# Down projection's biases in a mixture of experts: added once to each token's row of sums instead of once in each block

## The chip, the cores and the metric

One core of one Trainium2 chip runs the whole program in one launch. The metric is the device time of that launch in microseconds. The core has TensorE (PE, with its weight loads shown apart as PEld), VectorE (DVE), ScalarE (ACT), GpSimd (POOL), SyncE (SP), and 16 DMA engines that serve the queues of SP, ACT and POOL.

## What is computed

The reference is two transformer blocks on 512 tokens of width 1024. The change lies in the last part, the mixture of experts (32 experts, each token goes to 4 of them, hidden width 1024):

```python
def moe_ffn(h, w_router, b_router, w_gate_up, b_gate_up, w_down, b_down):
    logits = jnp.dot(h, w_router, ...) + b_router
    top_logit, top_idx = lax.top_k(logits, TOP_K)              # TOP_K = 4
    gate = jax.nn.softmax(top_logit, axis=-1)
    ...                                                        # slots: 128 rows of one expert make a block
    def expert_block(args):
        tok, g, e = args
        xb = h_pad[tok]
        gu = xb @ w_gate_up[e] + b_gate_up[e]
        y = clamped_swiglu(gu) @ w_down[e] + b_down[e]
        return y * g[:, None].astype(y.dtype)
    y = lax.map(expert_block, ...)
    out = jnp.zeros((n_tok + 1, d), y.dtype).at[slot_tok].add(y.reshape(n_slots, d))
    return out[:n_tok]
```

A token's output is therefore the sum over its four experts of gate times (down projection plus b_down of that expert), and the bias part of it is the gates' sum of b_down, which depends on the routing alone.

## The kernel before

Everything is float32. A product is made of three: each operand is split into a high part (ACT, a copy rounded to fp32r) and a low part (DVE, the rest), and high·high, low·high and high·low are added up in PSUM. That is the `k` and `part` loops of `half` in `experts_pe`.

**Up to the loop.** The two blocks' layers take the time up to about 1240 us. Then the router's results are turned into lists: DVE works out each slot's place (`tail_dve`), PE's 16 products of group "lists" put tokens and gates of all slots into one tile, DVE copies them out as `list_tok` and `list_gate`, and POOL (`experts_pool`) gathers the first two blocks' rows with an indirect DMA (`rows_of`) and fetches lists (`take_list`, two tiny copies and a `drain`). A DRAM tensor `acc_dram` (in the trace: acc_rows) holds a row of sums for every token; five DMAs of 512 KB of zeros, issued by POOL near the start of the program, clear it. `b_split` is the biases of all experts (gate, up and down, 3072 columns, experts as partitions, high parts in 32 rows and low parts in the next 32), which `bias_sp`, `bias_act` and `bias_pool` make long before the loop. `bias_pool` also clears the four row buffers `xgy`, of which the first two (`xg`) take gathered rows and the last two (`y_sb`) a block's results.

**The loop.** It runs 32 blocks of 128 slots, two per pass (`Fori(0, n)`), on all five engines at once. A block's weights are six 1024x512 quarters of two halves each: 12 halves of 1 MB. For each half, SP loads it into `raw` (a ring of 6), ACT copies the high part into `w_split` (a ring of 4, so it waits until PE is through with the half four before: semaphore half_used), DVE subtracts to get the low part, and PE does 12 products of 512 columns (`half`). The order of the halves is the table TURN: two halves each of gate and up for the first 512 hidden columns and then the second 512, and the down projection's halves between them: `run(6)`, `run(7)`, `run(10)` and `run(11)` are the down projection's, in PSUM banks 4 and 5, `run(8)` and `run(9)` already the next block's first.

Around the halves stand these steps, each waiting for another engine:

- `bias(j, s)` begins the sum in bank j with the expert's bias row: one product of 512 columns of `sel` (ones in the rows of the expert, made by `select` on DVE) with `b_split`. There are six a block: j = 0 to 3 for gate and up, 4 and 5 for down.
- After `run(5)` PE waits for the previous block's results to have been taken out of banks 4 and 5 (`ye_ready`), does `bias(4)` and `bias(5)`, and then waits until the first half of the hidden rows, turned, is split (`t_out`, DVE's `turned_low` with output hidden_T) before `run(6)`. Before `run(10)` it waits for the second half of them in the same way.
- ACT's queue has, besides the 12 high parts, two tanh (act_buf, L1360 and L1369), the high parts of turned rows (L1338), and `take_out` (L1341), which scales banks 4 and 5 by the gate into `y_sb`.
- DVE's queue has, besides the 12 low parts (L1381), the clamped gates (L1397), the hidden rows (L1401 to L1405), the low parts of turned rows (L1387) and `select` (L1392).
- POOL gathers rows for the block after the next and adds `y_sb` into `acc_dram` by an indirect DMA.

At the end SP reads `acc_dram` back and the last layer's norm follows.

Of the kernel before, what the change touches and what calls it, by code (L numbers as in the profile page):

```python
# [19 lines left out]
F32 = mybir.dt.float32  # L20
F32R = mybir.dt.float32r
# [12 lines left out]
P = 128  # L34
# [194 lines left out]
def build(nc, io):  # L229
    ctx = ExitStack()  # L230
    with ctx:
# [42 lines left out]
        empty = early.enter_context(nc.sbuf_tensor("empty", [P, LISTS], F32))  # L274
        early.close()
# [23 lines left out]
        xg, y_sb = xgy[:, 0:2, :], xgy[:, 2:4, :]  # L299
        b_raw = xgy[0:2 * E_N, 0:3, :].rearrange("p a b -> p (a b)")  # L300
# [128 lines left out]
        CV = Groups(nc, ctx, "cv", [0, 1, 2], [f"w{i}" for i in range(DK)] + ["pos", "be", "lists"])  # L429
        CA = Groups(nc, ctx, "ca", [3, 6, 7], [f"t{i}" for i in range(8)])  # L430
# [92 lines left out]
        SHIFT, SQ_SUM, LAST_GAINED, R_COL, CHOSEN, DIAG = range(1, 7)  # L523
# [3 lines left out]
        gate_exp, gate_d = sem("gate_exp"), sem("gate_d")  # L527
# [27 lines left out]
        def tail_pe(pe, mm):  # L555
# [237 lines left out]
            m.then_inc(CV.full, 1)  # L793
            experts_pe(pe, mm)
# [139 lines left out]
        def tail_dve(dve, inverse, rope):  # L934
# [222 lines left out]

            x = full(CV, "lists")[:, 0:2 * LISTS].rearrange("p (c b) -> p c b", c=2)
# [5 lines left out]
            dve.sem_inc(CV.free, 1)  # L1164
            experts_dve(dve)
# [39 lines left out]
        def bias_pool(pool):  # L1205
            pool.drain()
            nc.gpsimd.memset(b_split[2 * E_N:P, :].bitcast(F32), 0.0)
            pool.drain()
            pool.wait_ge(bias_high, 1)
            nc.gpsimd.tensor_tensor(b_split[E_N:2 * E_N, :], b_raw[E_N:2 * E_N, :],  # L1210
                                    b_split[E_N:2 * E_N, :].bitcast(F32), ALU.subtract).then_inc(bias_split, 1)
            pool.drain()
            nc.gpsimd.memset(xgy[:], 0.0)
            pool.drain()

        def experts_sp(sp):
# [3 lines left out]
            sp.wait_ge(CA.full, CA.n)  # L1220
# [22 lines left out]
        def experts_pe(pe, mm):  # L1243
# [18 lines left out]
            def half(n_, slot, j, q, s, inc=1):  # L1262
                rows = xgT[:, s] if j < 4 else hTe[:]
                w = wsp[:, slot % SPLIT]
                pe.wait_ge(high, n_ + 1)
                for k in range(4):
                    at_ = (4 * q + k) * P
                    for part in range(2):
                        mm(ps[:, j, :], rows[:, part, at_:at_ + P], w[:, 0, k * S:(k + 1) * S], False, False)
                pe.wait_ge(low, n_ + 3)  # L1270
                for k in range(4):
                    at_ = (4 * q + k) * P
                    m = mm(ps[:, j, :], rows[:, 0, at_:at_ + P], w[:, 1, k * S:(k + 1) * S], False,
                           q == 1 and k == 3)
                m.then_inc(used, inc)

            pe.wait_ge(bias_split, 1)
# [8 lines left out]
            with pe.Fori(0, n) as i:  # L1286
                for s in range(2):
# [23 lines left out]
                    bias(4, s)  # L1311
                    bias(5, s)
# [14 lines left out]
        def experts_act(act):  # L1327
# [16 lines left out]
            act.wait_ge(CA.full, CA.n)  # L1344
# [31 lines left out]
        def experts_dve(dve):  # L1376
# [62 lines left out]
        def experts_pool(pool):  # L1439
# [6 lines left out]
            pool.wait_ge(acc_init, 16 * (ACC_ROWS // P))  # L1446
# [30 lines left out]
            take_list(0, 0)  # L1477
            with pool.Fori(0, n) as i:
# [1148 lines left out]
        def _(pool):  # L2627
            def constants_in():
# [6 lines left out]
                for t in range(ACC_ROWS // P):  # L2635
                    pool.dma_start(acc_dram[1 + t * P:1 + (t + 1) * P, :], io["zeros"]).then_inc(acc_init, 16)
# [192 lines left out]
```

## Time and profile before

| | |
|---|---|
| median of 3 runs | 2475.66 us (2474.69 to 2476.12) |
| the profiled execution | 2474.83 us |
| its span in the trace | 2473.0 us |
| PE busy | 2400.4 us, 97% of the span |
| DVE busy | 2020.5 us, 82% |
| ACT busy | 1319.3 us, 53% |
| POOL busy | 689.3 us, 28% |
| weight load of PE (PEld) busy | 1938.1 us, 78% |
| the loop of 32 blocks | from about 1269 us to 2431 us |

The 1.8 us between span and time lie outside the traced span. An engine's busy time is the union of its instructions. Busy PE is not PE at its peak, since its products overlap: one of 512 columns is shown 0.39 us long and the next begins 0.23 us after it. The page's chain of the work that ended last puts 87% on PE; it follows an engine's own instructions wherever the wait ahead of one is small.

### The profile page before, as it was taken

How to read it: one execution, taken by the hardware profiler on the slowest of the kernel's cores; microseconds unless marked ns; L12 is line 12 of the kernel's file. 1: busy time of each engine (PE TensorE's matmuls, PEld its weight loads, DVE VectorE, ACT ScalarE, POOL GpSimd, SP SyncE). 2: the span in 40 equal slices, each digit the busy share in tenths (PEclk: the TensorE clock that was granted, in tenths of full speed). 3: DMA queues.
4: the chain of work that ended last, by engine and by line, in shares of the span. 5: the costliest groups of instructions: out<-in, count | busy, mean ns of one | idle time of the engine just before them, and what ended most of it. 6: DMA issues, size and time to landing. Idle time of an engine off the chain costs nothing.

```text
span 2473.0 us, 31635 instructions
## 1 busy us (share of the span) xinstructions
PE 2400.4 (97%) x10905; PEld 1938.1 (78%) x10905; DVE 2020.5 (82%) x1839; ACT 1319.3 (53%) x1207; POOL 689.3 (28%) x409
## 2 busy tenths in 40 slices
PE   8999999999999999999969999999999999999995
PEld 7777788777877877887858888888888888888883
DVE  7787577576885796887379999999999999999994
ACT  4442223334423234425357777777777777777772
POOL 5343251333433423342322112211211221122120
PEclk9999999999999998999989999999999999999998
DMA  6232246221422672320099999999999999999992
GB/s 240 86 120 77 68 146 203 69 77 68 145 61 76 223 262 64 108 94 27 13 323 370 370 372 370 372 367 377 366 366 373 368 371 373 373 364 366 375 361 90
DMA packets 105989, 574.55 MB, mean 232 GB/s; under 512 B 15241, under 2 KB 15401, under 8 KB 55850
## 3 DMA queue, kind: packets, MB, share of 16 engines
q1 hardware_dynamic: 87770, 515.16, 55.7%
q0 software_dynamic: 17856, 58.25, 8.4%
q8 instruction: 47, 0.77, 0.1%
q14 instruction: 28, 0.23, 0.0%
q10 hardware_dynamic: 288, 0.14, 0.0%
HBM read 561.43 MB, written 26.22 MB: 238 GB/s over the span
## 4 chain that ended last, share of the span: by engine, by line
PE 87%; DVE 7%; DVEq 1%; DMA 1%; issue 1%; ACT 1%; POOL 1%; ACTq 0%; SPq 0%; POOLq 0%
PE ps L1585 84%; PE ps L1250 2%; DVE scr L2446 1%; DVE scr L2286 1%; DVEq L2448 1%; POOL pieces_split L2641 0%; DMA scr<-in_ada 0%; PE ps L695 0%; DVE mix L2337 0%; DVE y_split L2223 0%; DVE scr L2335 0%; DMA mix<-acc_rows 0%; DMA acc_rows<-rows,lst 0%; DVE w_split L1381 0%; DMA rows<-h_rows,slot_tokens 0%
## 5 line engine op out<-in xcount | busy, mean ns | idle before, releaser
L1381 DVE TENSOR_TENSOR w_split<-raw,w_split 128x2048 fp32r<-128x2048 f32 x386 | 877.7, 2288 | 52.9 <-ACT w_split L1332 41.8
L1585 PE MATMUL ps<-y_split,pieces_split 128*128 128x512 f32 x3600 | 846.3, 396 | 16.2 <-POOLq L2653 7.4
L1332 ACT ACTIVATE w_split<-raw 128x2048 fp32r<-128x2048 f32 x386 | 736.3, 1917 | 192.7 <-PE ps L1585 176.4
L1585 PEld LDWEIGHTS ps<-y_split,pieces_split 128*128 128x128 f32 x3600 | 680.4, 190 | 168.1 <-issue 26.3
L1585 PE MATMUL ps<-w_split,rows_T 128*128 128x512 f32 x3096 | 751.8, 394 | 0.1
L1585 PEld LDWEIGHTS ps<-w_split,rows_T 128*128 128x128 f32 x3096 | 575.2, 188 | 117.5 <-DVE rows_T L1387 0.6
L2641 POOL TENSOR_TENSOR pieces_split<-pieces,pieces_split 128x1024 fp32r<-128x1024 f32 x151 | 371.9, 2474 | 649.9 <-ACT pieces_split L1919 519.8
L1919 ACT ACTIVATE pieces_split<-pieces 128x1024 fp32r<-128x1024 f32 x144 | 151.3, 1058 | 426.9 <-PE ps L1585 395.9
L1585 PE MATMUL ps<-w_split,hidden_T 128*128 128x512 f32 x1536 | 363.5, 392 | 1.8 <-DVE hidden_T L1387 1.7
L1585 PEld LDWEIGHTS ps<-w_split,hidden_T 128*128 128x128 f32 x1536 | 285.9, 188 | 71.9 <-DVE hidden_T L1387 13.2
L1456 POOL COPY rows_i<-slot_tokens 128x1 int32 x32 | 56.6, 1768 | 370.0 <-PE ps L1250 369.5
L1585 PE MATMUL ps<-scr 128*128 128x128 f32 (+3 forms) x576 | 137.6, 387 | 2.7 <-DVEq L991 1.7
L1470 POOL DMA_INDIRECT acc_rows<-rows,lst x33 | 65.4, 1981 | 229.9 <-ACT rows L1341 229.9
L1585 PE MATMUL ps<-pieces_split,y_split 128*128 128x512 f32 (+1 forms) x672 | 126.1, 348 | 0.0
L1585 PEld LDWEIGHTS ps<-scr 128*128 128x128 f32 x576 | 86.8, 191 | 46.4 <-issue 33.6
L1585 PEld LDWEIGHTS ps<-pieces_split,y_split 128*128 128x128 f32 x672 | 106.7, 190 | 16.2 <-issue 1.4
L1461 POOL COPY lst<-slot_tokens 128x1 int32 (+1 forms) x34 | 10.7, 314 | 309.1 <-DMA acc_rows<-rows,lst 303.4
L1450 POOL DMA_INDIRECT rows<-h_rows,rows_i x32 | 88.9, 2778 | 26.8 <-issue 26.8
L2208 DVE RECIPROCAL scr<-scr 128x512 f32<-128x512 f32 (+1 forms) x20 | 63.9, 3193 | 24.8 <-ACT scr L1868 21.1
L1938 ACT ACTIVATE mix<-ps 128x512 f32<-128x512 f32 x32 | 19.0, 594 | 106.3 <-DVE ps L2262 106.3
L2446 DVE SCALAR_TENSOR_TENSOR scr<-scr,cond 128x1024 f32<-128x1024 f32 x56 | 70.6, 1282 | 5.2 <-DMA scr<-in_ada 2.7
L1585 PE MATMUL ps<-bias_split,expert_rows 128*128 128x512 f32 x193 | 70.4, 392 | 0.0
(276 smaller groups left out, 2062.6 us busy)
## 6 DMA issues: line engine op xcount, KB each, us to landing
raw<-in_w_moe SPq DMA_DIRECT2D x386, 1024.0 KB, 7.4
pieces<-in_pieces SPq DMA_DIRECT2D x181, 512.0 KB, 3.5
scr<-in_ada POOLq DMA_DIRECT2D x48, 512.0 KB, 5.5
scr<-in_ple SPq DMA_DIRECT2D x2, 1536.0 KB, 7.1
acc_rows<-in_zeros POOLq DMA_DIRECT2D x5, 512.0 KB, 11.1
h_rows<-shift_row SPq DMA_DIRECT2D x1, 2052.0 KB
hT<-in_xT SPq DMA_DIRECT2D x8, 256.0 KB, 5.6
h_rows<-scr POOLq DMA_DIRECT2D x4, 512.0 KB, 7.7
```

The costliest lines, as they stand in the source:

```text
L1250: m = pe.transpose(ps[:, bank, j * P:(j + 1) * P], src[:, j * P:(j + 1) * P], ident[:])
L1332: nc.scalar.activation(wsp[:, p % SPLIT, 0], raw[:, p % RAW, :], ACT.Copy).then_inc(high, 3 if p == 1 else 1)
L1381: nc.vector.tensor_tensor(wsp[:, p % SPLIT, 1], raw[:, p % RAW, :], wsp[:, p % SPLIT, 0].bitcast(F32), ALU.subtract).then_inc(low, 3 if p ...
L1450: nc.gpsimd.indirect_dma_start(out=xg[:, s, :], out_offset=None, in_=h2_dram[:, :], in_offset=bass.IndirectOffsetOnAxis(ap=index.bitcast(U ...
L1456: nc.gpsimd.tensor_copy(rows_i[:, s:s + 1], list_tok[:, bass.ds(b, 1)])
L1470: nc.gpsimd.indirect_dma_start(out=acc_dram[:, :], out_offset=bass.IndirectOffsetOnAxis(ap=lst[:, s, 0:1].bitcast(U32), axis=0), in_=y_sb[ ...
L1585: return pe.matmul(out, lhsT, rhs, start=start, stop=stop)
L1919: nc.scalar.activation(wps[:, n % A_SPLIT, 0], pieces[:, place_of(after, at_), :], ACT.Copy).then_inc(p_high, 1)
L2208: nc.vector.reciprocal(r, r)
L2286: last = nc.vector.scalar_tensor_tensor(o, x[:, 1 + w:1 + w + S], p_("conv_w", w * LRU_T + i), o, ALU.mult, ALU.add)
L2446: last = nc.vector.scalar_tensor_tensor(out, aring[slot], c, out, ALU.mult, ALU.add)
L2641: nc.gpsimd.tensor_tensor(wps[:, n % A_SPLIT, 1], pieces[:, place_of(layer, at_), :], wps[:, n % A_SPLIT, 0].bitcast(F32), ALU.subtract).t ...
```

## The change

- Before the loop DVE multiplies the one-hot table of chosen experts by the gates and sums over the four choices, which gives a token's gate for every expert (`gate_of`, twice side by side). PE turns it (group "gates", four transposes), ACT and DVE split it into `gate_T`.
- PE then makes eight tiles of 128 tokens by 512 columns: gates times down's biases, two products each (group "z0" to "z7", three banks in turn). ACT copies each out into memory that is not in use yet: the two `y_sb` buffers, `h_sb` and `act_buf`.
- POOL writes these four 128x1024 tiles to `acc_dram`. Four of the five DMAs of zeros near the start are gone; one stays, for the rows past the tokens.
- ACT, DVE and POOL wait in front of the loop for all five writes to `acc_dram` (`acc_init`), ACT and DVE since the loop writes over the staging memory.
- In the loop `bias(4)` and `bias(5)` are gone; the first product of `run(6)` and of `run(7)` begins the sum. The wait for `ye_ready` stays.
- `bias_pool` clears only the two `xg` buffers.

```diff
@@ bias_pool
-            nc.gpsimd.memset(xgy[:], 0.0)
+            nc.gpsimd.memset(xg, 0.0)
@@ tail_pe, after group "lists"
+            g = "gates"
+            ...
+            for t in range(ST):
+                m = pe.transpose(ps[0:2 * E_N, CV.bank(g), t * P:(t + 1) * P], gate_of[:, t].rearrange("p c e -> p (c e)"),
+                                 ident[:])
+            m.then_inc(CV.full, 1)
+            pe.wait_ge(bias_split, 1)
+            pe.wait_ge(route_ready, GATES_LOW)
+            for i in range(8):
+                g, t = f"z{i}", i // 2
+                pe.wait_ge(CA.free, CA.reusable(0, g))
+                out, at_ = ps[:, CA.bank(g), :], 2 * D + (i % 2) * S
+                mm(out, gate_T[0:2 * E_N, 0, t * P:(t + 1) * P], b_split[0:2 * E_N, at_:at_ + S], True, False)
+                mm(out, gate_T[0:E_N, 1, t * P:(t + 1) * P], b_split[0:E_N, at_:at_ + S], False, True).then_inc(CA.full, 1)
@@ tail_dve, ahead of the lists' copies
+            nc.vector.tensor_tensor(hot2, hot, value[:, :, 1:2].to_broadcast([P, ST * TOP, E_N]), ALU.mult)
+            dve.drain()
+            nc.vector.reduce_sum(gate_of[:, :, 0, :], hot2.rearrange("p (t k) e -> p t e k", k=TOP), AX.X)
+            dve.drain()
+            nc.vector.tensor_copy(gate_of[:, :, 1, :], gate_of[:, :, 0, :])
+            dve.drain().then_inc(route_ready, 1)
@@ ... and behind them
+            dve.wait_ge(gate_high, 1)
+            nc.vector.tensor_tensor(gate_T[0:E_N, 1, :], ps[0:E_N, CV.bank("gates"), :],
+                                    gate_T[0:E_N, 0, :].bitcast(F32), ALU.subtract).then_inc(route_ready, 1)
@@ experts_pe
+                begins = j >= 4 and q == 0
                 ...
-                        mm(ps[:, j, :], rows[:, part, at_:at_ + P], w[:, 0, k * S:(k + 1) * S], False, False)
+                        mm(ps[:, j, :], rows[:, part, at_:at_ + P], w[:, 0, k * S:(k + 1) * S], begins and k + part == 0, False)
                 ...
                     pe.wait_ge(ye_ready, b + 1)
-                    bias(4, s)
-                    bias(5, s)
                     pe.wait_ge(t_out, 3 * b + 4)
@@ experts_act, ahead of the loop
-            for p in range(2):
-                high_part(p, p, (raw_in[p], 16))
+            high_part(0, 0, (raw_in[0], 16))
+            act.wait_ge(CV.full, CV.done(0, "gates"))
+            nc.scalar.activation(gate_T[0:2 * E_N, 0, :], ps[0:2 * E_N, CV.bank("gates"), :], ACT.Copy).then_inc(gate_high, 1)
+            high_part(1, 1, (raw_in[1], 16))
+            for i in range(8):
+                act.wait_ge(CA.full, CA.done(0, f"z{i}"))
+                nc.scalar.activation(acc_begin[i // 2][:, (i % 2) * S:(i % 2 + 1) * S], ps[:, CA.bank(f"z{i}"), :],
+                                     ACT.Copy).then_inc(CA.free, 1)
+                if i % 2:
+                    act.drain().then_inc(z_out, 1)
             for q in range(2):
                 turned_high(xgT[:, 0, 0, q * S:(q + 1) * S], 6 + q, 1, q + 1)
+            act.wait_ge(acc_init, 16 * (ST + 1))
             with act.Fori(0, n) as i:
@@ experts_dve, ahead of the loop
+            dve.wait_ge(acc_init, 16 * (ST + 1))
@@ experts_pool
-            pool.wait_ge(acc_init, 16 * (ACC_ROWS // P))
             ...
             take_list(BLOCKS, 1)
             take_list(0, 0)
+            for t in range(ST):
+                pool.wait_ge(z_out, t + 1)
+                pool.dma_start(acc_dram[1 + t * P:1 + (t + 1) * P, :], acc_begin[t]).then_inc(acc_init, 16)
+            pool.wait_ge(acc_init, 16 * (ST + 1))
             with pool.Fori(0, n) as i:
@@ constants_in
-                for t in range(ACC_ROWS // P):
-                    pool.dma_start(acc_dram[1 + t * P:1 + (t + 1) * P, :], io["zeros"]).then_inc(acc_init, 16)
+                pool.dma_start(acc_dram[ROWS:ACC_ROWS, :], io["zeros"]).then_inc(acc_init, 16)
```

PE's queue in the loop, around `run(5)` to `run(8)` of the first of a pass's two blocks: before, the two down biases stand between the products with rows_T (`run(5)`) and those with hidden_T (`run(6)`).

```order
L1585 MATMUL ps<-w_split,rows_T 128x512 x4
L1310 REGISTER_ALU
L1585 MATMUL ps<-bias_split,expert_rows 128x512 x2
L1313 REGISTER_ALU
L1585 MATMUL ps<-w_split,hidden_T 128x512 x8
```

After the change:

```order
L1629 MATMUL ps<-w_split,rows_T 128x512 x4
L1343 REGISTER_ALU
L1344 REGISTER_ALU
L1629 MATMUL ps<-w_split,hidden_T 128x512 x8
L1304 REGISTER_ALU
```

The two products are gone and the two register steps, of the waits for `ye_ready` and `t_out`, now follow each other.

POOL's queue between the first gathers and the loop, with its waits, before (list_ready, acc_init and h2_out have all arrived when the first gather starts; the branch is the loop's head):

```order
L1450 DMA rows<-h_rows,slot_tokens 128x1024 [waits list_ready,acc_init,h2_out]
L1450 DMA rows<-h_rows,slot_tokens 128x1024
L1461 COPY lst<-slot_tokens 128x1
L1462 COPY lst<-slot_gates 128x1
L1461 COPY lst<-slot_tokens 128x1
L1462 COPY lst<-slot_gates 128x1
L1478 UNCONDITIONAL_BRANCH
```

After (acc_rows_begun is the semaphore `z_out`):

```order
L1490 DMA rows<-h_rows,slot_tokens 128x1024 [waits list_ready,h2_out]
L1490 DMA rows<-h_rows,slot_tokens 128x1024
L1501 COPY lst<-slot_tokens 128x1
L1502 COPY lst<-slot_gates 128x1
L1501 COPY lst<-slot_tokens 128x1
L1502 COPY lst<-slot_gates 128x1
L1520 DMA acc_rows<-rows 128x1024 [waits acc_rows_begun] x2
L1520 DMA acc_rows<-hidden 128x1024 [waits acc_rows_begun]
L1520 DMA acc_rows<-act_buf 128x1024 [waits acc_rows_begun]
L1522 UNCONDITIONAL_BRANCH [waits acc_init]
```

The four writes stand behind the two gathers and both fetches of lists, and the loop's head now waits for them.

ACT's queue ahead of the loop, before:

```order
L1332 ACTIVATE w_split<-raw 128x2048 x2
L1338 ACTIVATE rows_T<-ps 128x512 x2
L1350 UNCONDITIONAL_BRANCH
```

After:

```order
L1363 ACTIVATE w_split<-raw 128x2048 [waits half_in0,cv_full,ca_full]
L1379 ACTIVATE gates_by_expert<-ps 64x512 [waits cv_full]
L1363 ACTIVATE w_split<-raw 128x2048 [waits half_in1]
L1383 ACTIVATE rows<-ps 128x512 [waits ca_full] x4
L1383 ACTIVATE hidden<-ps 128x512 [waits ca_full] x2
L1383 ACTIVATE act_buf<-ps 128x512 [waits ca_full] x2
L1369 ACTIVATE rows_T<-ps 128x512 [waits t_full] x2
L1390 UNCONDITIONAL_BRANCH [waits acc_init]
```

Nine copies have come in, eight of them between the second weight half and the first turned rows, and a wait at the loop's head.

## Rows read from the trace of the kernel before

**Rows 1.** Busy time by engine in ten stretches of 106 us, 1340 to 2400: sum
```profile
sum 1060.00, PE 1060.00 PEld 871.78 DVE 1011.66 ACT 790.30 POOL 219.18; mean PE 106.00 PEld 87.18 DVE 101.17 ACT 79.03 POOL 21.92
```
**Rows 2.** Timeline of PE, one block: start, us, instructions
```profile
2000.99 1.03 PE L1250 MATMUL ps<-ident,rows 128*128 128x128 f32 x8
...
2016.41 0.61 PE L1585 MATMUL ps<-bias_split,expert_rows 128*128 128x512 f32 x2
2016.87 5.60 PE L1585 MATMUL ps<-w_split,hidden_T 128*128 128x512 f32 x24
...
2028.56 5.73 PE L1585 MATMUL ps<-w_split,hidden_T 128*128 128x512 f32 x24
...
2037.08 1.03 PE L1250 MATMUL ps<-ident,rows 128*128 128x128 f32 x8
```
**Rows 3.** Timeline of PE's weight loads, same block; brackets: idle before, and releaser
```profile
2016.65 5.40 PEld L1585 LDWEIGHTS ps<-w_split,hidden_T 128*128 128x128 f32 x24
...
2028.56 3.50 PEld L1585 LDWEIGHTS ps<-w_split,hidden_T 128*128 128x128 f32 x16 [0.36 <-DVE hidden_T L1387]
```
**Rows 4.** Timeline of DVE, same block
```profile
2003.14 2.29 DVE L1381 TENSOR_TENSOR w_split<-raw,w_split 128x2048 fp32r<-128x2048 f32 x1 [0.65 <-ACT w_split L1332]
...
2015.91 0.69 DVE L1387 SCALAR_TENSOR_TENSOR hidden_T<-ps,hidden_T 128x512 fp32r<-128x512 f32 x1
2016.78 2.29 DVE L1381 TENSOR_TENSOR w_split<-raw,w_split 128x2048 fp32r<-128x2048 f32 x1 [0.19 <-ACT w_split L1332]
...
2027.83 0.68 DVE L1387 SCALAR_TENSOR_TENSOR hidden_T<-ps,hidden_T 128x512 fp32r<-128x512 f32 x1
```
**Rows 5.** Timeline of ACT, same block
```profile
2001.19 1.92 ACT L1332 ACTIVATE w_split<-raw 128x2048 fp32r<-128x2048 f32 x1
...
2013.83 0.64 ACT L1369 ACTIVATE act_buf<-act_buf 128x512 f32<-128x512 f32 x1 [1.44 <-DVE act_buf L1397]
...
2014.84 3.71 ACT L1332 ACTIVATE w_split<-raw 128x2048 fp32r<-128x2048 f32 x2
```
**Rows 6.** Waits from 1340 to 2400: us in total, times, longest
```profile
PEld ps L1585 <- DVE hidden_T L1387: 10.2, 30, 0.4
```
**Rows 7.** Timeline of all engines ahead of the loop and at its head
```profile
1236.58 4.03 ACT L920 ACTIVATE scr<-ps,small 128x512 f32<-128x512 f32 x6 [0.17 <-PE ps L764]
...
1254.62 0.21 DVE L1159 TENSOR_SCALAR empty<-ps 128x50 f32<-128x50 f32 x1 [2.78 <-PE ps L1585]
...
1255.92 1.91 ACT L1332 ACTIVATE w_split<-raw 128x2048 fp32r<-128x2048 f32 x1 [0.52 <-DMA raw<-in_w_moe]
...
1257.72 3.12 POOL L1450 DMA_INDIRECT rows<-h_rows,slot_tokens  x1 [0.30 <-issue]
...
1262.04 1.94 PE L1250 MATMUL ps<-ident,rows 128*128 128x128 f32 x8 [7.45 <-DMA rows<-h_rows,slot_tokens]
...
1264.53 7.08 PE L1585 MATMUL ps<-w_split,rows_T 128*128 128x512 f32 x24
...
1268.01 0.18 POOL L1461 COPY lst<-slot_tokens 128x1 int32<-128x1 int32 x1 [5.71 <-issue]
...
1269.02 1.92 ACT L1332 ACTIVATE w_split<-raw 128x2048 fp32r<-128x2048 f32 x1 [4.41 <-PE ps L1585]
...
1270.97 2.29 DVE L1381 TENSOR_TENSOR w_split<-raw,w_split 128x2048 fp32r<-128x2048 f32 x1 [5.64 <-ACT w_split L1332]
```
**Rows 8.** A DMA issue in POOL's timeline; then DMAs: count, KB each, median us to landing
```profile
1240.94 0.84 POOL L1443 DMA_DIRECT2D h_rows<-scr  x1 [0.53 <-ACTq L923]
...
rows<-h_rows,slot_tokens POOLq DMA_INDIRECT x1, 9.9
...
mix<-acc_rows SPq DMA_DIRECT2D x4, 512.0 KB, 5.2
...
h_rows<-scr POOLq DMA_DIRECT2D x4, 512.0 KB, 7.7
...
acc_rows<-in_zeros POOLq DMA_DIRECT2D x5, 512.0 KB, 11.1
```

More of the change, by code:

```diff
@@ L274, in build @@
         empty = early.enter_context(nc.sbuf_tensor("empty", [P, LISTS], F32))
+        gate_of = early.enter_context(nc.sbuf_tensor("gates_by_token", [P, ST, 2, E_N], F32))
+        gate_T = early.enter_context(nc.sbuf_tensor("gates_by_expert", [P, 2, S], F32R))
         early.close()
@@ L299, in build @@
         xg, y_sb = xgy[:, 0:2, :], xgy[:, 2:4, :]
+        acc_begin = y_sb[:, 0, :], y_sb[:, 1, :], h_sb[:], act_buf[:, 0:2, :].rearrange("p a b -> p (a b)")
         b_raw = xgy[0:2 * E_N, 0:3, :].rearrange("p a b -> p (a b)")
@@ L428, in build @@
         BA = Groups(nc, ctx, "ba", [4, 5, 6, 7], ba_order)
-        CV = Groups(nc, ctx, "cv", [0, 1, 2], [f"w{i}" for i in range(DK)] + ["pos", "be", "lists"])
-        CA = Groups(nc, ctx, "ca", [3, 6, 7], [f"t{i}" for i in range(8)])
+        CV = Groups(nc, ctx, "cv", [0, 1, 2], [f"w{i}" for i in range(DK)] + ["pos", "be", "lists", "gates"])
+        CA = Groups(nc, ctx, "ca", [3, 6, 7], [f"t{i}" for i in range(8)] + [f"z{i}" for i in range(8)])
         DV = Groups(nc, ctx, "dv", [0, 1, 2, 3, 4, 5], [f"t{i}" for i in range(8)])
@@ L522, in build @@
         route_ready, route_full = sem("routing_ready"), sem("routing_full")
-        SHIFT, SQ_SUM, LAST_GAINED, R_COL, CHOSEN, DIAG = range(1, 7)
+        SHIFT, SQ_SUM, LAST_GAINED, R_COL, CHOSEN, DIAG, GATES, GATES_LOW = range(1, 9)
         SHIFT_SUM, R_SUM, LOGITS = range(1, 4)
@@ L526, in build @@
         h2n_ready, h2_out = sem("h2n_ready"), sem("h2_out")
-        gate_exp, gate_d = sem("gate_exp"), sem("gate_d")
+        gate_exp, gate_d, gate_high, z_out = sem("gate_exp"), sem("gate_d"), sem("gate_high"), sem("acc_rows_begun")
         be_ready, np_ready = sem("be_ready"), sem("np_ready")
@@ L793, in tail_pe @@
             m.then_inc(CV.full, 1)
+            g = "gates"
+            pe.wait_ge(CV.free, CV.reusable(0, g))
+            pe.wait_ge(route_ready, GATES)
+            for t in range(ST):
[10 more added lines that the diff above has]
+                mm(out, gate_T[0:E_N, 1, t * P:(t + 1) * P], b_split[0:E_N, at_:at_ + S], False, True).then_inc(CA.full, 1)
             experts_pe(pe, mm)
@@ L1164, in tail_dve @@
             dve.sem_inc(CV.free, 1)
+            dve.wait_ge(gate_high, 1)
+            nc.vector.tensor_tensor(gate_T[0:E_N, 1, :], ps[0:E_N, CV.bank("gates"), :],
+                                    gate_T[0:E_N, 0, :].bitcast(F32), ALU.subtract).then_inc(route_ready, 1)
+            dve.drain().then_inc(CV.free, 1)
             experts_dve(dve)
@@ L1219, in experts_sp @@
             sp.wait_ge(CV.full, CV.done(0, "pos"))
-            sp.wait_ge(CA.full, CA.n)
+            sp.wait_ge(CA.full, CA.done(0, "t7"))
             def expert(b):
```

3 lines of the change are left out of this document (1 added, 2 removed).

## The prediction

> **What bounds the kernel now.** I read the page's busy times first, then the loop in stretches, then one block engine by engine, then what runs ahead of the loop. The change takes 64 products from PE (2 in each of 32 blocks) and adds work and a wait in front of the loop, so two questions decide: what sets a block's period, and what sets the moment the loop begins.
>
> By the busy times PE looks like the bound: 97% of the span in the table, and in the loop it is busy in every microsecond, with DVE at 1011.66 of 1060 [rows 1]. But a busy PE hides small waits. A block repeats after 36.09 us (2000.99 to 2037.08 [rows 2]), so follow one period back from where PE does wait. Ahead of `run(10)`, at 2028.56, the weight load stood idle for 0.36 us until DVE's second hidden_T was there [rows 3]; that happens in every block: 30 times in 1060 us, 10.2 us in all [rows 6]. Now the chain behind that wait:
>
> - DVE's hidden_T runs from 2027.83 to 2028.51 [rows 4], and PE loads 0.05 us later.
> - DVE has worked without a pause since 2016.78, where it had waited 0.19 us for ACT's high part [rows 4].
> - That high part is the first of the two at 2014.84. ACT has been busy since its tanh at 2013.83, which had waited 1.44 us for DVE's clamped gate, L1397 [rows 5].
> - DVE has again worked without a real pause since 2003.14, where it had waited 0.65 us for ACT [rows 4], for the high part begun at 2001.19 [rows 5].
> - That one waits for PE to leave the half four before, `run(0)`. Its last product overlaps the transposes that begin at 2000.99 [rows 2], and ACT starts 0.20 us after that. `run(0)` follows `run(11)` and `run(10)` of the block before without a gap, and `run(10)` had waited for DVE.
>
> This is a closed ring through DVE, ACT and a short piece of PE (`run(10)`, `run(11)`, one bias product, `run(0)`), and its length is the 36.09 us. **The two down biases are not on it.** They stand on PE between `run(5)` and `run(6)`, in the stretch from 2001 to 2028 where PE runs beside DVE's chain and arrives early.
>
> **The change in the loop.** Two bias products take 0.46 us of PE (2016.41 to 2016.87 [rows 2]). If PE were the bound that would be 0.46 x 32 = 14.7 us. What is late next? Right behind them, `run(6)` needs DVE's first hidden_T, which ends at 2015.91 + 0.69 = 2016.60, and PE loads its first weights at 2016.65 [rows 3, 4]. The two products just fill that wait. Without them PE stands idle there for all but 0 to 0.05 us of the 0.46. What little is left is lost at `run(10)`, where PE waits anyway. No other member of the ring starts from PE's work between: the high parts for the last halves are early (DVE does not wait for one of them up to 2027.83 [rows 4]). So I put the loop's gain at **0**, with bounds 0 and -14.7 us, and choose by the wait in all blocks [rows 6]. DVE's and ACT's queues in the loop are unchanged, POOL's too; DMA moves the same bytes.
>
> **The change ahead of the loop.** Step by step, on the clock of the profiled execution:
>
> - DVE's three new instructions ahead of the lists' copies (a multiply over 512 columns, a sum over 512 and a copy of 128) are bounded by three 512-column ones of 0.69 us [rows 4], 2.1 us. They fit the 2.78 us in which DVE waits for PE's lists up to 1254.62 [rows 7]: 0. Without that cover they would cost their 2.1 us.
> - PE's four transposes and ACT's and DVE's split of the gates: PE is idle there until 1262.04 [rows 7]. ACT's copy goes ahead of the second high part at 1255.92, and delays it by about 0.1 us. DVE's low part of the gates comes at about 1256.0, so DVE's first low weights slip by 1.4 us, which PE does not need before its first half at 1264.53 [rows 7].
> - PE's 16 products from about 1257 and ACT's eight copies from about 1258. Six copies of this size took 4.03 us [rows 7], so eight take 5.4 us: until 1263.4. PE turns the first rows only when the banks are free, at 1263.5 in place of 1262.04: 1.5 us later. By itself this would move the loop by 1.5 us.
> - POOL writes the four tiles. It stands behind two gathers and both list fetches. The second fetch ran at 1268.01, after 5.71 us in which POOL stood still behind the drain of the first [rows 7]. The trace names no releaser, but the second gather, issued at 1257.72 [rows 7], landed 9.9 us later [rows 8], at 1267.6, so I take the gather as the cause and the hold as staying. POOL is then free at 1268.3. The tiles have all been ready since about 1263.5. An issue takes 0.84 us, and up to 0.53 lies between two [rows 8]; with 1.1 us from one to the next the last is issued at 1268.5 + 3 x 1.1 = 1271.8.
> - The last landing: the trace has no write of this kind, so bounds. Four plain reads of 512 KB on an otherwise idle chip landed in 5.2 us, four writes of 512 KB by POOL, adding, in 7.7 us, five DMAs of zeros in 11.1 us [rows 8]. I take 7.7: same issuer, direction and size. So `acc_init` is complete at 1279.5 (bounds 1277.0 and 1282.9).
>
> The Trainium skill (DMA: Bandwidth & Descriptors, Anatomy of one DMA) puts a transfer at about 2 us plus its bytes over 436 GB/s; for the four tiles together that is an estimate of 6.8 us from 1268.5, so 1275.3, and the sum would be 4.2 us lower than mine. By that rule one of them is an estimate of 3.2 us; the trace does not agree for the writes that add, at 7.7 us each.
>
> The wait then holds ACT, whose first high part in the loop ran at 1269.02, and DVE, whose first low part ran at 1270.97 [rows 7]. Queued behind ACT's wait are all high parts, so PE runs dry after the two halves begun at about 1266. **That is a delay of 1279.5 - 1269.0 = 10.5 us.** Does the loop catch up? In the first block DVE and ACT have the same queues and nearly no pause to give up, and from the second block on the ring sets the pace, so all of it stays to the end. It could grow by some 1.5 us: straight after idle time PE took 7.08 us for 24 products [rows 7] where the loop's take 5.60 [rows 2], and it will be idle again; I put this at 0, since in the first block the products wait for DVE's low parts. POOL's shorter clearing and its four fewer issues near the start each stand ahead of a longer wait of POOL for ACT and are worth 0.
>
> **Sum.** 2474.83 (the profiled execution, of which 2473.0 is span) + 0 (loop) + 10.5 = 2485.3. The median of the runs is 0.8 above the profiled one: **2486.1 us**. By the bounds of the landing: 2483.6 to 2489.5.
>
> **The rivals.**
>
> - *PE is the bound after all.* The place is the weight load at 2028.56. If DVE's hidden_T comes earlier once PE is earlier, all 0.46 us of a block come back: 2486.1 - 14.7 = 2471.4, faster than before, and by more than 0.2% once the delay at the head is under 9.7 us. For it speaks the busy time [rows 1] and that the wait there is only 0.36 us. Against it: the ring above, in which nothing starts earlier. Half of the gain would give 2478.8.
> - *The head's wait is short.* POOL's hold of 5.71 us goes away or has to do with code or weights rather than the gather. The last tile is then issued at about 1265.5 and lands at 1271 to 1276: a delay of 2 to 6.5 us, 2477.7 to 2482.2.
> - *The writes crawl* beside the weight loads, as the zeros did or worse: `acc_init` at 1283 to 1286, 2489.7 to 2492.7.
> - *The change does less than it says*, if the loop lost its two products but the period grew because `run(6)` begins a sum where another engine still reads the bank: `ye_ready` is waited for as before, so there is no such place.
>
> **How the numbers follow.** The likeliest case, no gain in the loop and a delay of 8 to 14 us, has 0.68. The short wait has 0.15, of which half ends within 0.2% (4.95 us, about what a measurement of this kernel can tell from no change) and half slower. PE as the bound has 0.12: 0.07 of it faster by over 0.2%, 0.05 within. Crawling writes have 0.05. That makes faster 0.07, within 0.2% 0.13, slower 0.80. The range leaves out the lower part of the PE rival and the far end of the slow writes: 2477.5 to 2490.5.
>
> **What would show it.** Right: the same 36.1 us from block to block, a wait of PE for DVE's hidden_T ahead of `run(6)` of about 0.4 us that was not there, and a longer one (0.4 to 0.8 us) ahead of `run(10)`; ACT's first high part of the loop at about 1279, released by a DMA to acc_rows; POOL's first such issue at about 1268. Wrong: a period of 35.6 us; or the loop's head before 1274. The forecast falls if DVE's chain is not what holds PE at `run(10)`, or if POOL's four writes are done before PE has used up the first two halves.

## The result, and the profile after

| | before | changed |
|---|---|---|
| median | 2476.12 us (5 runs, 2474.69 to 2477.44) | 2487.10 us (5 runs, 2486.04 to 2488.37) |
| profiled execution | 2474.83 us, span 2473.0 | 2488.37 us, span 2486.6 |
| loop, block to block | 36.11 us | 36.11 us |

The changed kernel takes 1.005 times as long (95% interval 1.0039 to 1.0061): 11.0 us more, where 10.4 were forecast. The period is the distance of the starts of the same eight row transposes many blocks apart, divided by the blocks between (the prediction's 36.09 came from one block). For the changed kernel, its PE timeline at two places 27 blocks apart: (2374.84 - 1399.77) / 27 = 36.11.

```profile
1399.77 1.03 PE L1282 MATMUL ps<-ident,rows 128*128 128x128 f32 x8
...
2374.84 0.93 PE L1282 MATMUL ps<-ident,rows 128*128 128x128 f32 x7
```

**The loop.** The wait that the prediction asked for is there. First the waits of the changed kernel's weight loads over 1060 us (total, times, longest), then one block of its PE timeline and weight loads, which answer to [rows 2, 3, 6]:

```profile
PEld ps L1629 <- DVE hidden_T L1427: 27.0, 59, 0.5
```
```profile
2005.17 5.31 PEld L1629 LDWEIGHTS ps<-w_split,hidden_T 128*128 128x128 f32 x24 [0.46 <-DVE hidden_T L1427]
2005.17 5.73 PE L1629 MATMUL ps<-w_split,hidden_T 128*128 128x512 f32 x24
...
2029.35 5.35 PEld L1629 LDWEIGHTS ps<-w_split,hidden_T 128*128 128x128 f32 x24 [0.50 <-DVE hidden_T L1427]
```

Before, PE waited for hidden_T 30 times, once a block, 10.2 us in all. Now it waits twice a block, 59 times and 27.0 us: 0.46 us ahead of `run(10)` (2005.17) and 0.50 us ahead of `run(6)` (2029.35), where the two bias products had stood. The extra 16.8 us of waiting over 29 blocks are 0.58 us a block; the products were 0.46.

**The head of the loop.** The changed kernel's timeline of all engines, which answers to [rows 7]:

```profile
1255.27 0.21 DVE L1187 TENSOR_SCALAR empty<-ps 128x50 f32<-128x50 f32 x1 [1.08 <-PE ps L1629]
...
1257.10 10.67 PE L1629 MATMUL ps<-bias_split,gates_by_expert 64*128 64x512 f32 x16 [1.44 <-issue]
...
1258.33 1.94 POOL L1490 DMA_INDIRECT rows<-h_rows,slot_tokens  x1 [0.30 <-issue]
...
1264.49 0.19 POOL L1501 COPY lst<-slot_tokens 128x1 int32<-128x1 int32 x1 [0.70 <-issue]
...
1265.39 1.17 POOL L1520 DMA_DIRECT2D acc_rows<-rows  x2 [0.60 <-issue]
...
1267.81 0.60 ACT L1383 ACTIVATE act_buf<-ps 128x512 f32<-128x512 f32 x1 [0.84 <-PE ps L1629]
...
1268.46 1.97 PE L1282 MATMUL ps<-ident,rows 128*128 128x128 f32 x8 [0.69 <-ACT act_buf L1383]
1268.73 0.54 POOL L1520 DMA_DIRECT2D acc_rows<-act_buf  x1 [1.66 <-ACTq L1386]
...
1270.99 6.24 PE L1629 MATMUL ps<-w_split,rows_T 128*128 128x512 f32 x24
...
1281.61 3.71 ACT L1363 ACTIVATE w_split<-raw 128x2048 fp32r<-128x2048 f32 x2 [10.54 <-DMA acc_rows<-act_buf]
...
1283.55 2.29 DVE L1421 TENSOR_TENSOR w_split<-raw,w_split 128x2048 fp32r<-128x2048 f32 x1 [11.76 <-ACT w_split L1363]
```

ACT's first high part in the loop starts at 1281.61 in place of 1269.02, released by the DMA of the last tile: 12.6 us later. That distance stays through all 32 blocks. Here is the end, before first and then changed: SP's read of the rows of sums moved by 12.59 us, the last norm's root by 13.52.

```profile
2440.27 1.76 SPq L1502 DMA_DIRECT2D mix<-acc_rows  x4
...
2448.97 5.08 PE L1515 MATMUL ps<-ident,mix 128*128 128x128 f32 x32 [17.39 <-DMA mix<-acc_rows]
...
2460.96 0.60 ACT L1528 ACTIVATE act_buf<-ps 128x512 f32<-128x512 f32 x1 [1.89 <-PE ps L1585]
```
```profile
2452.86 1.76 SPq L1546 DMA_DIRECT2D mix<-acc_rows  x4
...
2461.20 6.37 PE L1559 MATMUL ps<-ident,mix 128*128 128x128 f32 x32 [16.92 <-DMA mix<-acc_rows]
...
2474.48 0.60 ACT L1572 ACTIVATE act_buf<-ps 128x512 f32<-128x512 f32 x1 [3.18 <-PE ps L1629]
```

So of the 13.6 us between the two spans 12.6 arise ahead of the loop, 0 in it and 1.0 behind it: PE's 32 transposes took 6.37 us in place of 5.08 while the rows landed 0.36 us sooner. That microsecond is not the change's: in the traces of kernels with this same tail these transposes take from 5.08 us to 6.52 (`e1_no_down_bias` below). The profiled execution is also the longest of the five of the changed kernel; the medians differ by 11.0.

### The profile page after: what moved, and what is told of

It reads as the page before. It is cut to its first block, busy times and chain, and to the rows that moved or that the text cites. A ratio compares the mean times of both kernels' runs of the same rounds, so it can differ in the third digit from the quotient of the medians.

```text
span 2486.6 us, 31569 instructions
## 1 busy us (share of the span) xinstructions
PE 2413.1 (97%) x10861; PEld 1931.1 (78%) x10861; DVE 2021.5 (81%) x1843; ACT 1324.9 (53%) x1216; POOL 686.5 (28%) x409
## 4 chain that ended last, share of the span: by engine, by line
PE 76%; DVE 12%; issue 4%; ACT 2%; DVEq 2%; DMA 2%; POOL 1%; ACTq 0%; SPq 0%; POOLq 0%
PE ps L1629 74%; DVE w_split L1421 3%; ACT w_split L1363 2%; PE ps L1282 1%; DVE scr L2490 1%; DVE scr L2330 1%; DVEq L1444 1%; DVEq L2492 1%; DMA scr<-in_ada 1%; DVE hidden L1445 1%; DVE act_buf L1437 1%; DVE rows_T L1427 1%; DMA acc_rows<-act_buf 1%; DVE hidden_T L1427 1%; POOL pieces_split L2684 0%
## 5 line engine op out<-in xcount | busy, mean ns | idle before, releaser
L1501 POOL COPY lst<-slot_tokens 128x1 int32 (+1 forms) x34 | 10.2, 299 | 303.3 <-DMA acc_rows<-rows,lst 302.6
L1369 ACT ACTIVATE hidden_T<-ps 128x512 fp32r<-128x512 f32 x64 | 37.8, 590 | 46.8 <-PE ps L1282 46.8
```

Of the source, the lines that this page charges most:

```text
L1369: nc.scalar.activation(dst, src, ACT.Copy, scale=scale).then_inc(t_high, 1)
```

## The experiments

Two theories of the loop stood against each other: the ring (PE's saved time turns into waiting) and PE as the bound. Two of the head: the biases' writes are slow by themselves, or they stand behind weight loads. All times are medians; the ratio is to the kernel before, timed on the same chip as the run. Its median there was 2475.61 us for `e1` to `e4`, 2475.22 for `e5`, `e7` and `e8`, and 2475.36 for `e9` and `e10`, so kernels of different groups are compared by their ratios.

| run | median (range, runs) | ratio [95%] | period |
|---|---|---|---|
| `e1_no_down_bias` | 2476.79 (2472.77 to 2478.80, 11) | 1.0001 [0.9992, 1.0010] | 36.11 |
| `e2_head_only` | 2486.24 (2485.34 to 2486.55, 5) | 1.0043 [1.0029, 1.0056] | 36.12 |
| `e3_shorter_ring` | 2469.66 (2466.87 to 2470.55, 8) | 0.9975 [0.9965, 0.9986] | 35.95 |
| `e4_shorter_ring_no_down_bias` | 2468.12 (2464.72 to 2470.14, 6) | 0.9968 [0.9956, 0.9980] | 35.86 |
| `e5_loads_held` | 2480.49 (2478.05 to 2482.80, 11) | 1.0020 [1.0011, 1.0029] | 36.11 |
| `e7_biases_at_the_end` | 2477.62 (2473.63 to 2480.22, 11) | 1.0007 [0.9998, 1.0016] | 36.11 |
| `e8_end_and_shorter_ring` | 2462.12 (2460.05 to 2465.39, 5) | 0.9945 [0.9931, 0.9958] | 35.68 |
| `e9_ring_35_67_products_kept` | 2467.47 (2465.75 to 2468.82, 6) | 0.9967 [0.9955, 0.9979] | 35.88 |
| `e10_ring_35_67_no_down_bias` | 2463.66 (2459.18 to 2466.33, 5) | 0.9945 [0.9932, 0.9959] | 35.68 |

### The loop's half and the head's half alone

`e1_no_down_bias` is the kernel before without the two products, and with nothing in their place:

```diff
             def half(n_, slot, j, q, s, inc=1):
+                begins = j >= 4 and q == 0
...
-                        mm(ps[:, j, :], rows[:, part, at_:at_ + P], w[:, 0, k * S:(k + 1) * S], False, False)
+                        mm(ps[:, j, :], rows[:, part, at_:at_ + P], w[:, 0, k * S:(k + 1) * S], begins and k + part == 0, False)
...
                     pe.wait_ge(ye_ready, b + 1)
-                    bias(4, s)
-                    bias(5, s)
```

> The kernel before without the two bias products for down in the blocks, and nothing in their place: the output lacks down's biases. It is the loop's part of the change alone. Ring theory (a block's 36.1 us are set by a ring through VectorE and ScalarE on which these products do not stand): no change, 2476 us within 1, and TensorE waits for hidden_T twice a block, about 0.4 us each. Rival (TensorE is the bound): 0.46 us a block come back, 14.7 us in all, 2461 us.

`e2_head_only` is the changed kernel with the two products back:

```diff
-                begins = j >= 4 and q == 0
+                begins = False
...
                     pe.wait_ge(ye_ready, b + 1)
+                    bias(4, s)
+                    bias(5, s)
```

> The changed kernel with the two bias products for down put back into the blocks: down's biases are counted twice. It is the head's part of the change alone. Ring theory: as the changed kernel, 2487 us within 1, since the products cost nothing in the loop. Rival: 14.7 us slower than the changed kernel, 2502 us.

Measured: 1.0001 without the products, so 64 products of PE less, 14.7 us of its busy time, are worth nothing within 2.5 us; and 2486.24 with the head alone, against 2487.10 for the whole change. The weight loads of `e1_no_down_bias` wait as often and as long as those of the changed kernel (waits of 1050 us):

```profile
PEld ps L1584 <- DVE hidden_T L1386: 27.0, 58, 0.5
```

So PE does not bound this loop, and what made the change slower is its head.

### The ring made shorter

If the ring holds PE, a shorter ring must bring time even with all the products. `e3_shorter_ring` is the kernel before with two moves. PE does `run(0)`, whose end lets ACT go on, ahead of the bias product of the same bank; and ACT does the tanh of half 7 behind the high part of half 8 (the turned rows too):

```diff
                     pe.wait_ge(act_ready, 2 * b + 2)
-                    bias(1, s)
-                    run(0)
+                    run(0, True)
+                    bias(1, s, False)
...
                     for p in range(HALVES):
-                        if p == 8:
-                            turned_high(hTe[:, 0, 0:S], 6, 1, 3 * b + 4, 0.5)
                         act.wait_ge(used, half_at(b, p) - SPLIT + 1)
                         high_part(half_at(b, p), FIRST + p, raw_landed(b, p))
...
-                        if p == 7:
+                        if p == 8:
+                            turned_high(hTe[:, 0, 0:S], 6, 1, 3 * b + 4, 0.5)
                             act.wait_ge(glu_ready, 2 * b + 2)
```

> The kernel before with the ring shortened and the products for down kept: on ScalarE the high part of a block's ninth half goes ahead of the tanh and the turned rows (VectorE waits 0.19 us for it now), and on TensorE the bias product of bank 1 goes behind the first half's products (0.23 us less up to the end of that half). Ring theory: the ring loses 0.42 us a block, but TensorE by itself, with all six bias products, needs 36.1 less the 0.20 us that it loses at its one wait, so the period falls to 35.9 and the time by 6 to 7 us, to 2469.5. Rival (TensorE is already the bound): no change, 2476.

`e4_shorter_ring_no_down_bias` makes the same two moves in `e1_no_down_bias`.

> The same two moves, and the bias products for down left out as in the first of these kernels (the output lacks down's biases). Ring theory: now TensorE has room, the ring's whole 0.42 us a block show, 13.4 us in all, 2462.5: the products for down are worth 6 to 7 us here and nothing in the first pair. Rival (TensorE is the bound in both pairs): 14.7 us less than the kernel above it.

The first came out as expected, 2469.66 at a period of 35.95. The second did not: 35.86 and 2468.12, against an expected 2462.5. PE's products had become worth 0.09 us a block, not 0.2. One block of `e4_shorter_ring_no_down_bias`, ACT, DVE and PE:

```profile
2009.08 1.92 ACT L1331 ACTIVATE w_split<-raw 128x2048 fp32r<-128x2048 f32 x1 [1.11 <-PE ps L1583]
...
2010.90 0.58 ACT L1337 ACTIVATE hidden_T<-ps 128x512 fp32r<-128x512 f32 x1
...
2011.51 0.69 DVE L1385 SCALAR_TENSOR_TENSOR hidden_T<-ps,hidden_T 128x512 fp32r<-128x512 f32 x1
...
2012.26 5.33 PEld L1583 LDWEIGHTS ps<-w_split,hidden_T 128*128 128x128 f32 x24 [0.53 <-DVE hidden_T L1385]
```

I had closed a second ring. The high part of half 8 waits for PE to be through with `run(4)` (1.11 us, 2009.08), and now the turned hidden rows stand behind it on ACT; DVE's hidden_T and `run(6)` follow without a gap. That ring goes through PE from `run(6)` of one block to `run(4)` of the next, then through ACT and DVE back to `run(6)`. It is 35.86 us long, whatever the tanh does. The test of it is `e10_ring_35_67_no_down_bias` below, where only the turned rows stand elsewhere and the period is 35.68.

So `e9_ring_35_67_products_kept` and `e10_ring_35_67_no_down_bias` leave the turned rows where they were, ahead of the high part of half 8, and move the tanh alone on ACT; PE's move of the bias product behind `run(0)` stays. The first is the kernel before with these two moves, the second `e1_no_down_bias` with them. ACT's part of the edit:

```diff
                             turned_high(xgT[:, 1 - s, 0, :], 6, 2, 3 * b + 3)
-                        if p == 7:
+                        if p == 8:
                             act.wait_ge(glu_ready, 2 * b + 2)
```

> The kernel before with the two moves of the run before (high part of the ninth half between turned rows and tanh on ScalarE, bank 1's bias product behind the first half), the products for down kept and nothing else changed. The ring would allow 35.67 us a block; TensorE with six bias products needs 35.86 to 35.89. Ring theory: TensorE is the bound, 6 to 7 us less than before, 2469, with no wait for hidden_T ahead of run(10). If the ring still sets the pace: 2462.

> The same without the two products for down (the output lacks down's biases). Ring theory: 35.67 us a block, 13.4 us less than before, 2462, as in the kernel with the biases at the end: so in this pair the products are worth 6 to 7 us where they were worth nothing in the kernel before. If TensorE was still the bound without them: all 14.7 us less than the kernel above, 2454.

Now the two products count. With them the period is 35.88 us, PE waits for no hidden_T at all in the stretch from 1340 to 2400 us, and PE is the bound; without them it is 35.68, the ring is the bound, and the wait is back (47 times, 12.7 us). PE's timeline in the first kernel, 26 blocks apart, and in the second, 27 blocks apart, and the second one's waits:

```profile
1424.00 1.03 PE L1250 MATMUL ps<-ident,rows 128*128 128x128 f32 x8
...
2356.79 1.03 PE L1250 MATMUL ps<-ident,rows 128*128 128x128 f32 x8
```
```profile
1390.41 1.03 PE L1250 MATMUL ps<-ident,rows 128*128 128x128 f32 x8
...
2353.78 1.03 PE L1250 MATMUL ps<-ident,rows 128*128 128x128 f32 x8
```
```profile
PEld ps L1584 <- DVE hidden_T L1386: 12.7, 47, 0.4
```

932.79 / 26 = 35.88 and 963.37 / 27 = 35.68: 0.20 us of the 0.46 come back, up to where the ring stops it, or 6.4 us over 32 blocks. In the medians it is 3.8 us; in the profiled executions the second kernel is 2.1 us behind when the first of these transposes run (1390.41 + 35.68 = 1426.09 against 1424.00), 1.1 of which it is at the loop's first block, and 3.0 ahead at the last. The expected 2469 and 2462 and the measured 2467.5 and 2463.7 differ by less than the runs of one kernel do (3.1 and 7.2 us from lowest to highest). The periods carry this reading, since the intervals of the two ratios overlap.

### The writes without loads ahead of them

`e5_loads_held` is the changed kernel, but SP holds the weight loads from half 3 of a block on until the rows of sums are begun (from the second block on this wait is always met):

```diff
                         sp.wait_ge(low, half_at(b, p) - RAW + 3)
+                        if p == 3:
+                            sp.wait_ge(acc_init, 16 * (ST + 1))
```

> The changed kernel, with one wait more: SyncE issues the loop's fourth weight load only when the rows of sums have all landed, so that three loads of 1 MB no longer stand in front of the four writes. If the 12.6 us from issue to landing of the last write are the weight loads' doing: it lands some 6 us earlier (512 KB writes took 7.7 us elsewhere), the loop begins at about 1276 in place of 1281.6, and the time falls by 5 to 6 us, to 2481.5. If the write itself takes that long: 2487, or later by what the held loads cost.

Measured 2480.49, 6.6 us less than the changed kernel (0.3% by the ratios, 1.0020 against 1.005, which is 7.4 us). The DMAs issued from 1265 to 1275 (count, KB each, median us from issue to landing), and then the timeline behind them:

```profile
acc_rows<-rows POOLq DMA_DIRECT2D x2, 512.0 KB, 4.3
acc_rows<-hidden POOLq DMA_DIRECT2D x1, 512.0 KB, 5.3
acc_rows<-act_buf POOLq DMA_DIRECT2D x1, 512.0 KB, 4.0
```
```profile
1268.15 0.54 POOL L1522 DMA_DIRECT2D acc_rows<-act_buf  x1 [2.01 <-ACTq L1388]
1270.41 7.40 PE L1631 MATMUL ps<-w_split,rows_T 128*128 128x512 f32 x24
...
1275.20 1.92 ACT L1365 ACTIVATE w_split<-raw 128x2048 fp32r<-128x2048 f32 x1 [4.72 <-PE ps L1631]
```

And the same DMAs in the changed kernel, issued from 1264 to 1270, with what the queues moved in that time (packets, MB, share of the 16 engines; q1 is SP's, q0 POOL's), and then the queues from 1270 to 1277:

```profile
q1 hardware_dynamic: 269, 1.98, 99.9%
...
acc_rows<-rows POOLq DMA_DIRECT2D x2, 512.0 KB, 11.2
acc_rows<-hidden POOLq DMA_DIRECT2D x1, 512.0 KB, 13.2
acc_rows<-act_buf POOLq DMA_DIRECT2D x1, 512.0 KB, 12.6
```
```profile
q1 hardware_dynamic: 257, 1.88, 65.0%
q0 software_dynamic: 267, 1.00, 35.0%
```

The last write lands 4.0 us after its issue without loads and 12.6 with them: 8.6 us are the loads'. In the changed kernel POOL's queue moved nothing in the 4.6 us from its first write (1265.39) to 1270, while the weight loads took the engines whole; from 1270 to 1277 it had 35.0% beside their 65.0%, and only then most of the engines' time (66.9% from 1277 to 1281, the loads 5.9%). Descriptors that come late do not explain the 4.6 us: with the loads held POOL's queue moves bytes between 1265 and 1266, at most 1.5 us after its first write was issued at 1264.46. With the loads held the loop's start is at 1275.20, and it is no longer the biases that release ACT but PE, which began its first halves at 1270.41 in place of 1264.53.

### The biases where nothing waits for them

`e7_biases_at_the_end` removes the products as the change does, but adds the gates' sum of biases behind the loop, while SP reads the rows of sums back. The rows begin with zeros as before. The gates' transposes and their split stay at the head:

```diff
         def final_pe(pe, mm):
+            pe.wait_ge(route_ready, GATES_LOW)
+            for k in range(DK):
+                g, at_ = f"z{k}", 2 * D + k * P
+                pe.wait_ge(DV.free, DV.reusable(0, g))
+                mm(ps[:, DV.bank(g), :], b_split[0:2 * E_N, at_:at_ + P], gate_T[0:2 * E_N, 0, :], True, False)
+                mm(ps[:, DV.bank(g), :], b_split[0:E_N, at_:at_ + P], gate_T[0:E_N, 1, :], False, True).then_inc(DV.full, 1)
...
             for k in range(DK):
+                dve.wait_ge(DV.full, DV.done(0, f"z{k}"))
+                nc.vector.scalar_tensor_tensor(hT[:, k, :], ps[:, DV.bank(f"z{k}"), :], ada[:, GT2 + k, 0:1],
+                                               hT[:, k, :], ALU.mult, ALU.add)
+                dve.drain().then_inc(DV.free, 1)
```

> Everything computed: the zeros, the gather and the loop's head as before, no bias products for down in the loop, and the gates' sum of biases made and added in the last microseconds, where TensorE waits 17 us for the rows of sums: 16 products with the biases as weights, eight additions to hT on VectorE. Ring theory: the head's delay is gone and the loop gives nothing, so the time is that of the kernel before, 2476 within 2. Rival (TensorE is the bound of the loop): 2461.

`e8_end_and_shorter_ring` adds to it the two moves of `e10_ring_35_67_no_down_bias`.

> The kernel with the biases at the end, and the ring shortened in another order: on ScalarE the high part of the ninth half goes ahead of the tanh, but behind the turned rows (with the turned rows behind it, as in the two runs with a shortened ring, a second ring through TensorE's products from run(6) to run(4), ScalarE's two copies and VectorE's hidden_T closes at 35.86 us); and the bias product of bank 1 behind the first half's products. Ring theory: period 36.09 - 0.42 = 35.67 us, 13.4 us less than before: 2462.5. If instead TensorE or another queue caps the loop at 35.86 as in the run before: 2468.5.

Moving the biases behind the loop leaves no loss that can be told from the kernel before (1.0007, interval 0.9998 to 1.0016) and still gains nothing, since the ring is the same. With the shorter ring it is 2462.12 us, the best of the kernels that compute everything: 0.9945 of the kernel before, 13.1 us less than its 2475.22 on the same chip, and by the ratios about 26 less than the changed kernel. `e10_ring_35_67_no_down_bias`, which leaves the biases out, has the same ratio. The timeline of PE and SP at the end of `e8_end_and_shorter_ring`:

```profile
2422.43 8.85 PE L1618 MATMUL ps<-gates_by_expert,bias_split 64*128 64x512 f32 x16 [1.35 <-DVEq L1560]
...
2429.43 1.76 SPq L1524 DMA_DIRECT2D mix<-acc_rows  x4
...
2437.63 6.49 PE L1543 MATMUL ps<-ident,mix 128*128 128x128 f32 x32 [6.36 <-DMA mix<-acc_rows]
```

The 16 products are over at 2431.3, and PE still waits 6.36 us for the rows: the sum of biases that cost 11 us ahead of the loop, with its copies and writes, costs nothing here that these runs can tell.

## Why the prediction came true, and where it did not

- **The loop: gain 0.** Right, and shown three ways: the period is the same, the wait ahead of `run(6)` is 0.50 us where "about 0.4" was said, and `e1_no_down_bias` has the kernel before's time. That it is the ring through DVE and ACT that holds PE is shown by `e9_ring_35_67_products_kept`, which only takes work out of that ring and gains 0.23 us a block with PE's work whole.
- **The rival "PE is the bound"** is out for this kernel. It was nearer than the busy table lets one see: PE's own length of a block with six biases is 35.88 us (`e9_ring_35_67_products_kept`), 0.23 under the ring's.
- **The head: 10.5 us by the sum, 12.6 in the profiled execution, 11.0 in the medians.** The forecast of the time is partly luck, because errors of both signs met in it: the last write was issued 3.1 us early, it took 4.9 us longer to land than the term for it, and ACT began 0.3 us after that.
- *POOL's hold* failed. I took the 5.71 us as staying, with the second gather landing 9.9 us after its issue. In the changed kernel it landed after 5.0, and POOL's wait was 0.70 us; it was ready to write at 1265.4, not 1268.5. The gather as the cause fits, since in both traces the second fetch follows its landing (1267.6 and 1268.01, 1263.3 and 1264.49), but its duration was no constant. The eleven traces fall into two groups. From the issue of the second gather to the second fetch there are 9.2 to 11.1 us in the six kernels with the head of before, and 6.1 to 6.3 in the five that split the gates there. `e7_biases_at_the_end` and `e8_end_and_shorter_ring` are among the five and have neither tiles nor their writes ahead of the loop, so these are not what shortened it. What the queues moved from 1262 to 1268 before (q1 is SP's, q0 POOL's):

```profile
q1 hardware_dynamic: 247, 1.84, 83.3%
q0 software_dynamic: 144, 0.29, 12.3%
```

  Before, nearly half of the gathers' 0.65 MB moved in this stretch, beside weight loads. In the changed kernel they had moved all of it by 1263 (0.64 MB from 1260 to 1263, beside 0.10 of loads). SP issued its next load 2.4 us after the second gather in all six kernels of the first group and 3.4 to 4.6 us after it in the five of the second. In every trace that load goes out 2.4 us after DVE's first low weights begin, and these slipped behind the low part of the gates: 1.6 us in the changed kernel (1259.31 against 1257.69), which the prediction put at 1.4 and took for harmless. So the slip very likely kept weight loads out of the gather's way, but no run moved the loads alone.
- *The tiles ready at 1263.5* failed. I had priced ACT's copies (0.67 us each) and not PE's products, which set the pace: 16 in 10.67 us, two per tile, with ACT waiting 0.84 us for each tile from the third on. The last tile was ready at 1268.4. The granted clock did most of this. PE's weight loads of these products, early and late:

```profile
1257.92 0.18 PEld L1629 LDWEIGHTS ps<-bias_split,gates_by_expert 64*128 64x128 f32 x1 [0.24 <-issue]
...
1263.38 0.28 PEld L1629 LDWEIGHTS ps<-bias_split,gates_by_expert 64*128 64x128 f32 x1 [0.44 <-issue]
```

  Up to 1258.34 (granted clock 1.00 from 1257 to 1258) one product's load began 0.42 us after the last one's, 0.18 of loading and 0.24 of pause. From 1259.06 on, at 0.50, it was 0.72 us. Sixteen at 0.42 would be over at 1263.8 and the last copy at 1264.4, an estimate from these rows, 0.9 us from the forecast.
- *Both together*: POOL came 3.1 us earlier than forecast and the last tile 4.9 us later. The forecast had POOL as the later of the two, so the last issue was early all the same, at 1268.73 against 1271.8, and now set by the tile.
- *The last landing* failed. I took 7.7 us from the writes of h_rows [rows 8], with 11.1 as upper bound from the zeros. It was 12.6, beyond both; only because the issue was early did the moment of landing, 1281.3, stay within the prediction's 1277.0 to 1282.9. What is disputed, the writes or the loads ahead of them, `e5_loads_held` settles: 4.0 us without loads. By this the mechanism of the rival "the writes crawl beside the weight loads" was at work, though not its time (1283 to 1286). The condition of the rival "the head's wait is short", that POOL's hold goes away, came true as well, but its last issue at about 1265.5 did not, since the tiles were late. The hold and the landing were thus each named by a rival, and the measured time lies between the times of the two. What should have been priced is what SP has queued ahead of the writes: from 1264 to 1281 its queue moved 3.96 MB of weights (1.98, 1.88 and 0.10 in three stretches), the writes themselves 2.09.
- *PE's first rows*, expected 1.5 us late, were 6.4 us late (1268.46 against 1262.04), because they wait for the same products and copies. In the changed kernel this hid behind the writes; in `e5_loads_held` it sets the start of the loop, at 1275.20. Mending the writes alone could therefore not have brought the change to the time of before: 1.0020, interval 1.0011 to 1.0029.
- *DVE's three instructions are covered*: right. Its wait for the lists shrank from 2.78 to 1.08 us, and the next step ran 0.65 us later than before (1255.27 against 1254.62).
- **No catching up.** Right: 12.6 us at the first high part, 12.59 at the read of the rows.
- **The rule of the Trainium skill.** For one write of 512 KB it gave an estimate of 3.2 us (DMA: Bandwidth & Descriptors, Anatomy of one DMA). `e5_loads_held` shows 4.0 to 5.3 us, so the rule is near on free engines; in the changed kernel, behind loads, it is off by a factor of four. The same page (Queues, rings and completion order) says that a DMA engine takes turns between the queues for which it has work. The trace shows sharing of that kind from 1270 on (35.0% and 65.0%), but not from 1265.4 to 1270, where POOL's queue moved nothing although its first write was issued.

## What to carry to other kernels

An engine that is 97% busy need not be the bound: walk back from each of its short waits, and if the walk returns to itself one period earlier through other engines, work taken from the busy engine turns into waiting until that ring is shortened. Work whose result all engines await at a loop's head is paid in full if nothing there hides it; look first for a wait at the other end of the program that can. A slip that hides on its own engine can still move another queue's transfers, for better or worse. And price a DMA by what is queued ahead of it at that moment, not by the median of its like elsewhere.

## What the runs showed of the hardware that was not expected

The granted clock fell although PE was busy. The windows of the changed kernel, columns: the stretch, its length, busy share and instructions of PE, PEld, DVE, ACT and POOL, then the granted clock, the DMA share and GB/s:

```profile
1256.00:1257.00 1.00, 0.00 (x0) 0.00 (x0) 0.68 (x1) 1.00 (x2) 0.09 (x1) 1.00 0.97 410
1258.00:1259.00 1.00, 1.00 (x2) 0.39 (x2) 0.63 (x1) 0.63 (x2) 0.70 (x2) 0.69 1.00 426
1259.00:1260.00 1.00, 1.00 (x3) 0.50 (x2) 1.00 (x3) 0.60 (x1) 1.00 (x1) 0.50 0.99 418
1271.00:1272.00 1.00, 1.00 (x2) 0.82 (x3) 0.69 (x1) 0.06 (x1) 0.00 (x0) 0.50 1.02 430
1272.00:1273.00 1.00, 1.00 (x6) 0.80 (x5) 0.00 (x0) 0.00 (x0) 0.00 (x0) 0.99 1.00 418
```

PE had little to do up to 1257, and was then given the bias products without a pause. The clock went to 0.50, the lower of its two levels (1.2 GHz), and stayed there for the rest of them, though the profile calls PE busy; it came back at 1272, about a microsecond into the first half's products of 128 rows. At the lower level a product of 512 columns took 0.72 us (1.44 for a tile's two), where the loop's halves take 5.60 / 24 = 0.23 us each. The clock is only part of that: at 1.00 these products already took 0.42 us each, since each one's weight load came only after a pause of 0.24 us and not during the product before, as it does in the loop (there the loads fill 5.40 of the 5.60 us [rows 2, 3]). At the end of `e8_end_and_shorter_ring` 16 products of the same sizes took 8.85 us: the loads of the first ten came 0.42 us apart, with the clock at 1.00 up to 2426, the last ones 0.72 apart at 0.50. What in them let the clock fall, the 32 and 64 rows of the two forms or the gaps between them, no run told apart. The second thing not expected is the 4.6 us in which POOL's writes moved nothing beside SP's loads; why the engines gave them no turn is open.
